# Two transformer blocks on one core: another order of the prologue, and the filter sums on GpSimd

## The reference

```python
# modulation: six vectors, from two conditions
mod_x = silu_c @ w_mod[l] + b_mod[l]                 # w_mod is 1024 x 6144
hx = modulate(rmsnorm(x, p["norm_mix"]), sh_a, sc_a)  # first operand of all products with w_in
# the filters of the Hyena mixer: a small MLP with sines over positions, times a decay
h = h @ p["hy_w4"]; h = h * jnp.exp(-t * deltas)
h = h.reshape(L, HY_ORDER, HY_DIRS, HY_WIDTH)         # 2 orders, forward and backward
k_full = jnp.concatenate([h[:, :, 0], zeros, h[:0:-1, :, 1]], axis=0)
return jnp.fft.rfft(k_full, axis=0)
# the projections
q_x, k_x, v_x, hy_x = jnp.split(hx @ p["w_in"], cuts, axis=-1)
```

## Time and profile before

| | |
|---|---|
| median of 3 runs | 1685.37 us (1684.92 to 1685.61) |
| the profiled execution | 1684.08 us, its span 1682.3 us |
| TensorE busy | 1630.9 us of the span |
| VectorE busy | 987.5 us |
| ScalarE busy | 691.6 us |
| GpSimd busy | 142.8 us |
| mean granted TensorE clock | 0.994 |

### The profile page before, as it was taken

One profiled execution on the slowest core, in us unless ns is written; L12 is line 12 of the kernel. 1 busy time (PEld: TensorE's weight loads), 2 busy tenths in 40 slices (PEclk: granted clock), 3 DMA queues, 4 the chain that ended last, 5 costly groups with the idle time before them and its releaser, 6 DMA issues.

```text
span 1682.3 us, 18849 instructions
## 1 busy us (share of the span) xinstructions
PE 1630.9 (97%) x7214; PEld 1271.2 (76%) x7214; DVE 987.5 (59%) x1375; ACT 691.6 (41%) x1038; POOL 142.8 (8%) x152
## 2 busy tenths in 40 slices
PE   5999999999999999999999999999999999999997
PEld 2588765677888888888888786568877888888885
DVE  6985787775544334446788696665534553535252
ACT  4521465224443123336554588836434322212131
POOL 0221000252000000013000000222000100000001
PEclk9999999999999999999999999999999999999999
DMA  9544114423132333223341022335111322222221
GB/s 317 185 160 145 47 51 150 151 101 99 53 100 88 104 109 100 81 89 106 111 143 71 26 76 93 99 129 203 50 50 51 111 90 100 101 100 100 100 100 50
DMA packets 113833, 176.13 MB, mean 105 GB/s; under 512 B 3995, under 2 KB 56795, under 8 KB 113244
## 3 DMA queue, kind: packets, MB, share of 16 engines
q1 hardware_dynamic: 109452, 160.28, 28.2%
q0 software_dynamic: 4304, 14.81, 2.7%
HBM read 170.63 MB, written 4.46 MB: 104 GB/s over the span
## 4 chain that ended last, share of the span: by engine, by line
PE 81%; DVE 9%; ACT 4%; DMA 3%; issue 2%; SPq 1%; DVEq 0%; ACTq 0%
PE bank L899 17%; PE bank L901 16%; PE bank L900 16%; PE bank L936 6%; PE bank L937 6%; PE bank L941 5%; DMA weight_slots<-in_w_mod 2%; PE bank L1209 2%; PE bank L1129 1%; PE bank L1141 1%; PE bank L1339 1%; DVE weight_slots_lo L2363 1%; PE bank L1424 1%; DVE arena L2904 1%; PE bank L1536 1%
## 5 line engine op out<-in xcount | busy, mean ns | idle before, releaser
L3235 POOL TENSOR_TENSOR arena<-arena 128x512 f32<-128x512 f32 (+1 forms) x56 | 76.1, 1367 | 954.9 <-ACT arena L1641 951.1
L901 PE MATMUL bank<-hx_hi,weight_slots_lo 128*128 128x512 f32 x320 | 124.7, 390 | 0.0
L3190 DVE TENSOR_TENSOR weight_slots_lo<-weight_slots,weights_hi 128x2048 fp32r<-128x2048 f32 x30 | 67.4, 2289 | 96.6 <-ACT weights_hi L2322 96.6
L2322 ACT ACTIVATE weights_hi<-weight_slots 128x2048 fp32r<-128x2048 f32 x30 | 55.8, 1908 | 163.7 <-DMA weight_slots<-in_w_up 116.4
L1610 ACT ACTIVATE weights_hi<-weight_slots 128x2048 fp32r<-128x2048 f32 (+2 forms) x46 | 77.2, 1723 | 91.6 <-DMA weight_slots<-in_ffn_w_down 57.7
L900 PE MATMUL bank<-xn_lo,weights_hi 128*128 128x512 f32 x288 | 112.1, 389 | 0.0
L899 PE MATMUL bank<-sq_hi,weights_hi 128*128 128x512 f32 x256 | 99.6, 389 | 0.0
L900 PE MATMUL bank<-sq_lo,weights_hi 128*128 128x512 f32 x256 | 99.6, 389 | 0.0
L901 PE MATMUL bank<-sq_hi,weight_slots_lo 128*128 128x512 f32 x256 | 99.6, 389 | 0.0
L1596 ACT ACTIVATE arena<-bank 128x512 f32<-128x512 f32 (+2 forms) x99 | 49.0, 532 | 93.1 <-PE bank L901 46.4
L2363 DVE TENSOR_TENSOR weight_slots_lo<-weight_slots,weights_hi 128x2048 fp32r<-128x2048 f32 (+2 forms) x36 | 70.4, 1990 | 28.1 <-ACT weights_hi L1610 28.1
(11 more groups left out here) (451 smaller groups left out, 4091.5 us busy)
## 6 DMA issues: line engine op xcount, KB each, us to landing
weight_slots<-in_w_in SPq DMA_DIRECT2D x24, 1024.0 KB, 7.3
weight_slots<-in_ffn_w_up SPq DMA_DIRECT2D x22, 1024.0 KB, 6.6
weight_slots<-in_w_up SPq DMA_DIRECT2D x16, 1024.0 KB, 6.6
weight_slots<-in_w_down SPq DMA_DIRECT2D x16, 1024.0 KB, 6.4
weight_slots<-in_w_mod SPq DMA_DIRECT2D x14, 1024.0 KB, 10.0
arena<-in_w_mod POOLq DMA_DIRECT2D x32, 256.0 KB, 3.3
weight_slots<-in_w_out SPq DMA_DIRECT2D x8, 1024.0 KB, 7.5
weight_slots<-in_w_xkv SPq DMA_DIRECT2D x8, 1024.0 KB, 7.4
```

Source lines behind the costliest of these rows:

```text
L901: return mm(ps, ll, rh, start=False, stop=stop)
L2322: A(W_hi[:, s % 2, a:b], W[:, s % 2, a:b], ACT.Copy).then_inc(w_hi, 1)
L3190: V.tensor_tensor(W_lo[:, s % 2, a:b], W[:, s % 2, a:b], W_hi[:, s % 2, a:b].bitcast(F32), ALU.subtract).then_inc(w_lo, 1)
L3235: G.tensor_tensor(acc, acc, sq[i % 2][:, 0:width], ALU.add).then_inc(sq_added, 1)
```

## The change

It has three parts. SyncE issues modulation slabs 0 and 1 right behind the parameters, ahead of the constants, `neg_taps`, `hy_w4`, `delta` and `dft_k`, and x behind modulation slab 3 in place of ahead of everything. On TensorE the parts of the prologue stand in another order. And the sum of forward and backward filter goes from VectorE to GpSimd, with two buffers `hb` in turn.

```diff
+FILTER_ORDER = ((0, 1, 2, 3), (0, 2, 1, 3))
 def job_plan():
-    j += ["h1", "h2", "h3"]
+    j += ["h1", "h2", "h3", "mods_0"]
-    j += ["x_parts"] + pairs[0] + pairs[1] + ["norm_x", "mods_0"] + pairs[2] + pairs[3]
+    j += pairs[0] + pairs[1] + ["mods_1"] + ke[0][:2] + pairs[2] + pairs[3] + ke[0][2:] + ko[0]
+    j += ["x_parts", "modc_0", ke[1][0], "norm_x"] + ke[1][1:] + ko[1]
...
-        hb = tile(77)
+        hb = [tile(77), tile(71)]
```

On VectorE and GpSimd:

```diff
-                for i, t in enumerate(T_ORDER):
+                for i, t in enumerate(FILTER_ORDER[o]):
...
-                    V.tensor_tensor(hb, ps[:], dec[1], ALU.mult).then_inc(psum_free[jobs[b_] % 8], 1)
+                    back = hb[i % 2]
+                    if NT * o + i >= 2:
+                        dve.wait_ge(sem("filter_ready"), NT * o + i - 1)
+                    V.tensor_tensor(back, ps[:], dec[1], ALU.mult).then_inc(psum_free[jobs[b_] % 8], 1)
...
-                    link(V.tensor_tensor(pd, pf, hb, ALU.subtract))
-                    V.tensor_tensor(pf, pf, hb, ALU.add).then_inc(sem("filter_ready"), 1)
-                    dve.wait_ge(sem("filter_ready"), NT * o + i + 1)
-            ps = full(dve, "mods_1")
-            evicted(dve, "mods_0")
-            free(V.tensor_tensor(mod_row[0], mod_row[0], ps[:], ALU.add), "mods_1")
+                    V.tensor_tensor(pd, pf, back, ALU.subtract).then_inc(sem("filter_diff"), 1)
+                if o == 0:
+                    ps = full(dve, "mods_1")
+                    evicted(dve, "mods_0")
+                    free(V.tensor_tensor(mod_row[0], mod_row[0], ps[:], ALU.add), "mods_1")
+            for pair in SPECTRA[:4]:
+                spectrum_pair(*pair)
...
+            split_w("k", 0)
             dve.wait_ge(sem("silu_ready"), 1)
...
+            for o in range(2):
+                for i, t in enumerate(FILTER_ORDER[o]):
+                    pool.wait_ge(sem("filter_diff"), NT * o + i + 1)
+                    pf = Psum_f[o][:, t, :]
+                    G.tensor_tensor(pf, pf, hb[i % 2], ALU.add).then_inc(sem("filter_ready"), 1)
```

More of the change, by code:

```diff
@@ L452, in two_blocks @@
         xin = tiles(0, 8)
-        x_sq = tiles(16, 8)
-        x_parts = tile(16)
+        x_sq = tiles(25, 8)
+        x_parts = tile(33)
         Zdft, Zdft_lo = (parts(f"dft_z_{n}", a, 4).rearrange("p a c -> p (a c)").rearrange("p (t f) -> p t f", t=2)
@@ L697, in slab @@
                 put(s, k8(s), rows(w, c0, 512))
+            slab("mod", 0, io["w_mod"], 0)
+            slab("mod", 1, io["w_mod"], 512)
+            load(con[:], io["consts"], "con")
+            load(neg_taps[:], tables["neg_taps"], "neg_taps")
             for e in range(2):
@@ L948, in first_products, with modulation_slab @@
                          lambda k: pe.wait_ge(x_hi, operand_no[op, k] + 1), lambda k: operand(op, k), end, middle, at, width, lows)
[L950 to L964, removed]
+            def modulation_slab(ps, s):
+                w = landed("mod", s)
+                if s == 0:
+                    pe.wait_ge(sem("silu_ready"), 1)
+                for k in range(KD):
+                    g = 32 * (k % 4)
+                    ins = mm(ps[g:g + 32, :], silu[:, k, 6 - 2 * s:38 - 2 * s], w[:, k, :], start=s % 2 == 0 and k < 4,
+                             stop=s % 2 == 1 and k >= KD - 4, tile_position=(0, g))
+                if s == 0:
+                    ins.then_inc(sem("mod_read"), 1)
+                return ins
             def all_modulation_columns():
@@ L1033, in _, with modulation_pair, filter_heads @@
                 end(ins)
-            input_parts()
+            def modulation_pair(n):
+                ps = begin(f"mods_{n}")
+                for s in (2 * n, 2 * n + 1):
+                    ins = modulation_slab(ps, s)
+                end(ins)
+            modulation_pair(0)
+            def filter_heads(o, i):
+                for d in range(2):
+                    for t in T_ORDER[2 * i:2 * i + 2]:
+                        ps = begin(f"h4_{o}_{t}_{d}")
+                        e = t // 2
+                        end(mm(ps[:], hT[2][halves[e], P * (t % 2):P * (t % 2) + P],
+                               w4[halves[e], 512 * (2 * o + d):512 * (2 * o + d) + 512], start=True, stop=True))
@@ new lines, in spectrum @@
+            def spectrum(parity, o, c, m):
+                pe.wait_ge(sem("filter_ready"), NT * o + max(FILTER_ORDER[o].index(2 * parity + t) for t in range(2)) + 1)
+                src = (Psum_f if c == "re" else Diff_f)[o]
+                f0 = (256 if c == "im" else 0) + P * m
+                ps = begin(f"K{'EO'[parity]}{c}_{o}_{m}")
+                for t in range(2):
+                    ins = mm(ps[:], Kdft[:, 2 * parity + t, f0:f0 + P], src[:, 2 * parity + t, :], start=t == 0, stop=t == 1)
+                end(ins)
@@ L1048, in _ @@
[L1048 to L1062, removed]
+            for i in range(2):
+                filter_heads(0, i)
@@ new lines, in _ @@
+            modulation_pair(1)
+            loaded(pe, "dft_k")
+            for m in range(2):
+                spectrum(0, 0, "re", m)
+            for i in range(2):
+                filter_heads(1, i)
+            for m in range(2):
+                spectrum(0, 0, "im", m)
+            for o, c, m in SPECTRA[:4]:
+                spectrum(1, o, c, m)
+            input_parts()
+            all_modulation_columns()
+            for n, (o, c, m) in enumerate(SPECTRA[4:]):
+                spectrum(0, o, c, m)
+                if n == 0:
+                    input_squares()
@@ L1064, in _ @@
+            for o, c, m in SPECTRA[4:]:
+                spectrum(1, o, c, m)
             norm_sum("norm_ctx", CTX)
@@ L1692, in _ @@
             loaded(act, "neg_taps")
[L1694 to L1710, removed]
             def spectrum_out(o, c, m):
@@ L1726, in high_inputs @@
                     split_x(hx1_hi[:, k, :], hx1[:, k, :], mod[:, k, 0:1])
[L1728 to L1734, removed]
+            spectrum_out(*SPECTRA[5])
+            high_inputs(range(2))
+            spectrum_out(*SPECTRA[6])
+            high_inputs(range(2, 5))
             spectrum_out(*SPECTRA[7])
+            high_inputs(range(5, KD))
             norm_factor("norm_ctx", CTX)
```

79 lines of the change are left out of this document (42 added, 37 removed).

## The result

The changed kernel takes 1689.27 us (median of 16 runs, 1687.72 to 1691.1) against 1685.74 us for the kernel before (16 runs beside it, 1683.75 to 1689.07): a ratio of 1.0020, with an interval from 1.0014 to 1.0027. That is 3.5 us slower. The forecast was 7.5 us slower, and a time of 1692.9.

The account below looks back on a forecast made before the run. TensorE bounds the kernel, its first large product waiting on slab 3's transfer and in-order work behind it. 1684.08 + 5.5 (later product) + 2.0 (clock) = 1691.6, plus 1.3 median offset: 1692.9; range 1688.8 to 1695.5.

Parts of the forecast that it names:

- Slab 3 thus lands at 46.35 - 5.45 = 40.9: Transfer queue: with x's 2048 KB behind it, modulation slab 3 lands 5.45 us earlier, at 40.9; bounds 38.8 to 42.3.
- the slow stretch: Transfers at 223 GB/s, taken for the tables before the slabs; at 385 in the new order, 2.1 us less, 38.8.
- The 37.9 us of work behind it: TensorE from slab 3's arrival to the first large product, all in program order: 37.9 us, so product at 78.8.
- I take a low stretch of 4 us behind slab 3: half of it is lost, 2.0 us: TensorE's clock falls to half rate after idling around slabs 2 and 3, costing 2.0 us; bounds 0 and 2.6.
- The two pauses: TensorE idle from about 30 to slab 2 at 35.5, and again until slab 3 at 40.9: 4 to 5 us each.
- The base, 73.30: Start in us of TensorE's first large product in the shown execution of the kernel before.
- Every microsecond by which that product starts later is a microsecond of the whole until 250 us at least: TensorE is busy behind the first large product, so any shift of its start counts in full.
- The 1.3 us of the median over the profiled execution: Added to the sum of 1691.6, because the shown runs' median stood 1.3 us above the profiled execution: 1692.9.
- 1684.08 + 5.5 + 2.0 = 1691.6: Profiled time before, plus 5.5 us later first large product, plus 2.0 us clock loss: the changed kernel's own time.
- GpSimd's additions: Eight filter sums moved from VectorE, median 1292 ns each, last ending at 57.4; off the path, 5.8 us spare.
- Rival 3: Transfer time hangs on issue, not bytes ahead: slab 3 lands at 29.3, product 6.1 us earlier, 1679.3; chance 0.04.

Follow-up runs that it names:

- the delay experiment: The kernel before with 8 more f32 matmuls on TensorE ahead of the sum of the context's squares: ratio 1.0027, 4.5 us.
- best: Changed kernel with tables ahead of slabs 0 and 1, second pair behind the even spectra, x normalised before slab k's low part: 1681.41 us, 0.9970 of the kernel before.
- the first fillers: Changed kernel with 4 f32 matmuls into a free bank in each of TensorE's waits for slabs 2 and 3: ratio 1.0032.

## Why the prediction was right in its mechanism and wrong in its size

The time lies in the range given, and the forecast's direction and mechanism held. But the change cost 3.5 us where the sum said 7.5, so two of its terms were mis-sized.

- **"Slab 3 thus lands at 46.35 - 5.45 = 40.9"**: 39.40, 39.01 and 39.61, mean 39.34. This term was 1.6 us too late, still inside its bounds (38.8 to 42.3). Against the mean of the kernel before in four executions, 46.86, the slab came 7.5 us earlier, where the sum had 5.45. The prediction took x's bytes off at the plateau's rate, and nothing else. In the first pair of traces the bytes moved up to slab 3's landing were these (the last number is GB/s; the kernel before, then the changed one):

```profile
0.00:46.30 46.30, 27.46 (x122) 9.05 (x122) 31.64 (x59) 22.61 (x36) 0.44 (x6) 1.00 0.94 322
```
```profile
0.00:39.30 39.30, 17.89 (x76) 4.80 (x76) 17.91 (x39) 11.62 (x17) 5.52 (x10) 0.90 0.92 315
```

  That is 14.91 and 12.38 MB, 2.53 MB less, and x is 2.10 of them. All else that was issued up to slab 3 is the same in both, so the other 0.43 MB, 1.1 us at 385 GB/s, are of transfers issued behind it. Before, more of `lam`, the context and `rope` moved ahead of slab 3's end than of x in the changed kernel. The bound's reason, that the slow stretch would go, did not come true: it moved, and the mean rate from 5 to 39 us is 355 GB/s against 353. In the fourth execution of the kernel before that rate was 345; why the same queue differs from one execution to the next stays open.
- **The 37.9 us of work behind it**: 37.74 where the clock was full, in three executions. Right. It is the part that decides, and moving the pair alone gave it back.
- **"I take a low stretch of 4 us behind slab 3: half of it is lost, 2.0 us"**: the stretch behind 39.4 was 6.0 us long in two of three traces and absent in one; it cost 2.9, 2.9 and 0 us, a mean of 1.9. The size was right in the mean, and wrong as a thing that happens each time. The two pauses were 3.55 and 1.68 us long, shorter than the 4 to 5 us expected, and the clock fell in the first of them all the same. Half rate ahead of slab 3 costs nothing: in the changed kernel's second execution slab 2's records took 3.64 us and TensorE still waited 1.69 us afterwards.
- **The base, 73.30**: the one execution that the sum was made against had the earliest product of four, 0.6 us ahead of their mean. With the two terms above: forecast 80.8 - 73.30 = 7.5; measured 79.02 - 73.87 = 5.15. Of the 2.35 us between them, 2.1 are slab 3's landing and 0.3 the work behind it (12.7 us more than before, for 12.95).
- **"Every microsecond by which that product starts later is a microsecond of the whole until 250 us at least"**: the delay experiment bears it out up to 852 us, where 1.0 of 6.84 us is swallowed. In the first trace of the changed kernel the shift falls there from 5.84 to 5.41, the wait of 0.26 us being gone. The prediction then took the shift whole to the end. The rest behind the product is 1606.9 to 1611.5 us in the eleven rows of the table: 1607 with 3.4 us of low stretches in it, 1608.5 with 10.2, 1609 to 1611.5 with 13.6 to 17. In the three executions of the changed kernel it is 1608.1 in the mean, with 7.9 us low; in the four of the kernel before 1610.0, with 13.6 us low. That is the 1.9 us between 5.15 at the product and 3.2 in the spans: some 0.4 at the wait at 852, the rest by the clock (half of the 5.7 us, 2.8, is an upper estimate for it, since TensorE is not busy throughout).
- **The 1.3 us of the median over the profiled execution**: it stands on both sides of the difference, so it bears on the time alone. The changed kernel's profiled executions stand 0.3 to 0.6 below its median, not 1.3, and the second of the kernel before 1.8 above. The offset is not a property of profiling; the first execution shown happened to be a short one.

So the step that failed is the sum "1684.08 + 5.5 + 2.0 = 1691.6", 7.5 us over the kernel before, in two of its terms: slab 3's landing, 7.5 us earlier and not 5.45, and the carrying of the product's delay to the end, where 3.2 of 5.15 us arrived in the profiled spans. Against the mean of 1688.86 of the three profiled executions the 1691.6 is 2.7 too high: 1.6 from slab 3's landing, 0.2 from the work behind it, 0.9 from the rest behind the product (1609.0 against 1608.1). The offset adds 0.9. The clock's 2.0 was put on one side only, as if the kernel before had a fixed time; it has low stretches too. In its prologue they cost nothing at the product (26.95 to 27.1 us behind slab 3, with or without one), and behind the product they lengthen it more than the changed kernel in these executions. That the time still fell inside the range, 0.5 us above its lower end, is in part luck: that end was set for a full clock and an earlier slab together, and what came back behind the product had no term in it.

What stays open: whether the changed kernel's short low stretches behind the product in two of three executions (3.4 us, with 13.7 and more ahead of it) are tied to the long one ahead, or chance. Three executions don't tell, and if they are tied, 1 to 2 us of the prologue's loss are always given back. Over all kernels the time follows the product closely: from best (69.63, -4.24 against 73.87) to the first fillers (80.40, +6.53) the ratios go from -5.1 to +5.4 us.

GpSimd's additions took 1274 ns beside VectorE where the prediction had 1292, ended at 59.4 (57.4 forecast) and were awaited by nobody for more than 0.2 us. The Trainium skill, "GPSIMD Engine Reference", Elementwise, side-by-side cycle accounting, has 1.96 for the ratio of the two engines in a two-input addition, four times as wide; here it is 1274/692 = 1.84. Rival 3, a transfer time that hangs on the issue, fell: slab 3, issued at 25.14, took 14.22 us.

## What to carry to other kernels

On an engine that works its list in order, look at what stands behind each wait for a transfer, not only at when the transfer lands: here the slab came 7.5 us earlier and the product 5.2 us later. Give a transfer that comes earlier to work that can't start without it, and let work whose data is there go ahead of the wait.

A forecast of a few microseconds in 1685 needs more than one trace of the kernel before. Profile two or three executions, see which clock stretches are in all of them, and put a yes-or-no loss into both kernels' sums with its chance. Count the bytes moved up to a landing, not only those of the transfer that was taken away: what is issued behind can take its share.

## What the runs showed of the hardware

- **The clock's falls differ between executions of one program.** At 276.2 and at 1285.1 the granted clock was 0.50 (1.2 GHz) for 3.4 us in one execution and 1.00 (2.4 GHz) in another, with TensorE busy in both. Over the 50 executions beside the experiments (22 and 28) the kernel before took 1683.0 to 1689.4 us, at mean clocks of 0.996 down to 0.989. The Trainium skill, "TensorE: Matmul & The Clock Gate", The HAM clock gate, calls the number of slow matmuls at a start run-variable; the traces here agree, and show it for pauses in the middle of a kernel too.
- **The same pauses gave low stretches of different length.** Two waits of 3.55 and 1.7 us, with 16 records between them, came with a low stretch of 6.8 us in one execution of the changed kernel (30.6 to 37.5, over ahead of slab 3) and of 13.7 us in two (31.7 to 45.4 in the first). In the kernel before a wait of 3.44 or 3.45 us was followed by 3.4 us of half rate in two executions and by none in one.
- **A transfer's landing moved by up to 1 us** between executions with the same queue ahead of it: slab 3 was taken up at 46.35 and at 47.34.
- **Transfers issued behind another take a share before it has landed**: 0.43 MB more in the kernel before than in the changed one, by the bytes moved up to slab 3.
